# ScalarE copies for row sums, query rows and expert numbers; a search begun in the query blocks; gathers held for blocks of the down stage

## The reference, cut to what matters

```python
def peer(h, w_q, sub_keys, w_down, w_up):          # h: 256 tokens x 1024
    q = (ht @ w_q).reshape(T, 8, 2, 128)
    scores = einsum('thic,hikc->thik', q, sub_keys)   # 16 halves x 128 keys
    sv, si = lax.top_k(scores, 16)
    cand = sv[:, :, 0, :, None] + sv[:, :, 1, None, :]
    best, ci = lax.top_k(cand.reshape(T, 8, 256), 16)
    i1 = take_along_axis(si[:, :, 0], ci // 16, axis=-1)
    i2 = take_along_axis(si[:, :, 1], ci % 16, axis=-1)
    expert = (i1 * 128 + i2).reshape(T, 128)       # of 16384 experts
    gate = softmax(best, axis=-1).reshape(T, 128)
    hid = gelu(einsum('cd,ckd->ck', xb, w_down[eb]))
    return einsum('ck,ckd->cd', gb * hid, w_up[eb])
```

## Time and profile before

| what | value |
|---|---|
| median of 3 runs | 1516.04 us |
| the profiled execution | 1503.53 us |
| its span, first to last instruction | 1501.7 us |
| granted TensorE clock | 0.997 of full |
| busy: TensorE, VectorE, GpSimd, ScalarE | 1479.2, 892.0, 716.5, 473.2 us |
| moved through the DMA engines | 523.12 MB, mean 348 GB/s |

### The profile page before, as it was taken

One profiled execution on the slowest core, in us unless ns is written; L12 is line 12 of the kernel. 1 busy time (PEld: TensorE's weight loads), 2 busy tenths in 40 slices (PEclk: granted clock), 3 DMA queues, 4 the chain that ended last, 5 costly groups with the idle time before them and its releaser, 6 DMA issues.

```text
span 1501.7 us, 29008 instructions
## 1 busy us (share of the span) xinstructions
PE 1479.2 (98%) x10648; PEld 1440.7 (96%) x10648; DVE 892.0 (59%) x2921; ACT 473.2 (32%) x1184; POOL 716.5 (48%) x632
## 2 busy tenths in 40 slices
PE   8999999999999999999999999999999999999996
PEld 6889999999999999999978999999999999999996
DVE  1740999948885444444623449997588834444363
ACT  6663231248881000000055533121788500000001
POOL 6577033448994333333467831333699723332350
PEclk9999999999999999999999999999999999999998
DMA  7356999999999999999845679999999999999993
GB/s 257 133 204 235 332 339 364 409 408 342 383 389 407 416 416 417 416 417 415 360 150 200 211 244 351 349 407 408 367 375 385 383 416 415 416 417 416 417 404 141
DMA packets 126416, 523.12 MB, mean 348 GB/s; under 512 B 14816, under 2 KB 15072, under 8 KB 109536
## 3 DMA queue, kind: packets, MB, share of 16 engines
q1 hardware_dynamic: 56896, 240.27, 42.0%
q0 software_dynamic: 55296, 201.35, 34.3%
q10 hardware_dynamic: 14112, 80.04, 13.1%
HBM read 519.48 MB, written 1.05 MB: 347 GB/s over the span
## 4 chain that ended last, share of the span: by engine, by line
PE 94%; POOL 1%; DMA 1%; issue 1%; ACT 1%; DVE 1%; DVEq 0%; POOLq 0%; SPq 0%; ACTq 0%
PE ps L992 93%; POOL w_lo L605 1%; DMA spare<-in_wu 1%; PE ps L1000 1%; ACT hT_hi L707 0%; DMA raw<-in_wm 0%; DMA xs<-in_x 0%; ACT w_hi L692 0%; ACT arena L680 0%; DVE arena L1385 0%; DVE rtmp L1374 0%; DVE arena L1523 0%; POOL arena L630 0%; PE ps L1322 0%; PE ps L1120 0%
## 5 line engine op out<-in xcount | busy, mean ns | idle before, releaser
L992 PE MATMUL ps<-arena,raw 128*128 128x160 f32 (+1 forms) x2688 | 377.4, 299 | 0.2
L992 PE MATMUL ps<-arena,w_raw 128*128 128x160 f32 (+1 forms) x2688 | 377.3, 299 | 0.0
L992 PEld LDWEIGHTS ps<-arena,raw 128*128 128x128 f32 x2688 | 368.1, 190 | 0.7 <-issue 0.7
L992 PEld LDWEIGHTS ps<-arena,w_raw 128*128 128x128 f32 x2688 | 368.2, 190 | 0.0
L622 POOL DMA_INDIRECT arena<-in_up_rows,ret x192 | 188.1, 979 | 355.1 <-DVE oh_buf L1697 263.3
L622 POOL DMA_INDIRECT arena<-in_rows,ret x192 | 200.0, 1042 | 285.8 <-ACT ret L879 104.5
L1697 DVE SCALAR_TENSOR_TENSOR oh_buf<-arena,ret,oh_buf 128x1024 f32<-128x1024 f32 x126 | 161.8, 1284 | 227.9 <-DMA arena<-in_up_rows,ret 227.9
L605 POOL TENSOR_TENSOR w_lo<-raw,w_hi 128x1024 fp32r<-128x1024 f32 x80 | 194.0, 2436 | 90.8 <-PE ps L992 66.1
L992 PE MATMUL ps<-arena 128*128 128x160 f32 (+5 forms) x1336 | 184.5, 302 | 0.4 <-DMA spare<-in_wu 0.3
L992 PEld LDWEIGHTS ps<-arena 128*128 128x128 f32 (+2 forms) x1336 | 177.9, 189 | 4.0 <-issue 2.6
L1580 DVE SCALAR_TENSOR_TENSOR arena<-arena,ps 128x1024 f32<-128x1024 f32 x128 | 153.6, 1213 | 0.0
(11 more groups left out here) (149 smaller groups left out, 1780.6 us busy)
## 6 DMA issues: line engine op xcount, KB each, us to landing
raw<-in_wd SPq DMA_DIRECT2D x92, 512.0 KB, 6.8
w_raw<-in_wd SPq DMA_DIRECT2D x92, 512.0 KB, 7.6
raw<-in_wm SPq DMA_DIRECT2D x80, 512.0 KB, 3.4
low_rows<-in_wu SPq DMA_DIRECT2D x18, 1024.0 KB, 7.9
arena<-in_wu SPq DMA_DIRECT2D x18, 1024.0 KB, 7.9
arena<-in_wd SPq DMA_DIRECT2D x32, 512.0 KB, 4.9
raw<-in_wu SPq DMA_DIRECT2D x14, 1024.0 KB, 8.0
raw<-in_wu ACTq DMA_DIRECT2D x14, 1024.0 KB, 8.0
```

The source lines that it names most:

```text
L992: return nc.tensor.matmul(out, lhsT, rhs, start=start, stop=stop, skip_group_check=shared)
```

## The change

- The table `sel` and all products with it are gone. ScalarE's `take_rows` copies `gff` to both halves of banks 2 and 3 at block 8 of its loop; `take_more_picks` copies the numbers of the 32 tokens in four parts; VectorE's `find_more_rows` is gone.
- The sums of the sparse tokens are added to `xs` by VectorE. Partitions must match, so ScalarE first moves parts to the right partitions (`move_part`, and `sums_moved` for the 64 tokens) into two unused tiles `moved`. The up rows of the 32 tokens now come first (0 to 31); their moves stand in ScalarE's program between the loads of pairs 39 and 40 and between 47 and 48, the adds on VectorE behind row products 66 and 80. The adds of the 64 tokens stand at the layer's end. Tile 0 is turned back with transposes.
- The scores of the first 4 heads of tile 0 are computed ahead of query block 10 and taken by ScalarE behind its block 12; VectorE searches them at once. The search of tile 0 is split in two halves of 4 heads; dots are now spread over 20 places from the second half on, 44 of them (`EARLY`).
- Each of the first 53 gathers waits until TensorE has used a given number of down blocks (`pace`): gather q for q * 71 // 53. The pieces of numbers are handed over at blocks 4, 7, 20 and 25. The ring starts at slot 2, since slots 0 and 1 lie on tile 0's scores; gather 9 waits for these (`first_searched`).
- The gates are transposed at block 73 instead of 77, gate blocks begin at 76 instead of 80, and the dots left (52) spread over 48 blocks instead of 56 over 44.

```diff
-RING, IN_FLIGHT = 10, 5
+RING, IN_FLIGHT, RING_FIRST = 10, 5, 2
-IDS_AT = 77
-TAKE_AT = 26
-PIECES, PIECE_AT = 4, (18, 21, 24, 26)
-MORE_AT, MORE_TAKE_AT, MORE_GATES_AT = 28, 33, 40
+IDS_AT = 73
+TAKE_AT = 28
+PIECES, PIECE_AT = 4, (4, 7, 20, 25)
+EARLY_SCORES_BEFORE, EARLY_HEADS = 10, RH // 2
+SCORE_BANKS = (0, 1, 0, 1, 4, 5, 6, 7)
+MORE_AT, MORE_TAKE_AT, MORE_GATES_AT = 26, 34, 40
-G_FROM = 80
+G_FROM = 76
-SPARSE_FIRST, MORE_LAST = 18, 10
-EARLY, EARLY_PLACES = SPARSE_FIRST + MORE - MORE_LAST, 14
+SPARSE_FIRST, MORE_LAST = 26, 14
+EARLY, EARLY_PLACES = SPARSE_FIRST + MORE - MORE_LAST, 20
+def pace(q):
+
+    return q * (IDS_AT - 2) // (EARLY + RING - 1)
-    return (True, n - PICKS) if n >= PICKS else (False, n)
+    return (True, n) if n < MORE else (False, n - MORE)
+PARTS_AT, LAST_PART_AT = 5, 6
+PARTS_ADDED, LAST_PART_ADDED = 66, 80
+        moved = [at(HT_AT + i * DM, DM) for i in range(2)]
...
+                    if q < EARLY + RING - 1:
+                        pool.wait_ge(w_used, l * LAYER + MIX_BLOCKS + pace(q))
...
+                    if q == RING - 1:
+                        pool.wait_ge(first_searched, l + 1)
                     if q < ROWS and more and j == 0:
-                        pool.wait_ge(more_taken, l + 1)
+                        pool.wait_ge(more_taken, PARTS * (l + 1))
...
+                act.wait_ge(rinv_done, query_norm)
+                for b in range(Q_FROM + 12, MIX_BLOCKS):
+                    high(b)
+                    if b == Q_FROM + EARLY_SCORES_BEFORE + 2:
+                        take_scores(0)
+                        take_scores(1)
...
+                def take_rows():
+                    act.wait_ge(hng_done, l + 1)
+                    act.wait_ge(pair_found, PIECES * l + PIECES // 2)
+                    for half in range(2):
+                        nc.scalar.activation(h_rows[half * SPARSE:(half + 1) * SPARSE], gff[0:SPARSE],
+                                             ACT.Copy).then_inc(h_rows_done, 1)
...
-                blocks(act, load_up_between, UP_PAIRS, UP_PAIRS * UP_CYCLES, UP_PAIRS)
+                def move_part(i, to):
+                    nc.scalar.activation(to[SPARSE:DENSE_FROM], more_sums[i * MORE:(i + 1) * MORE],
+                                         ACT.Copy).then_inc(parts_moved, 1)
+
+                blocks(act, load_up_between, UP_PAIRS, UP_PAIRS * PARTS_AT, UP_PAIRS)
+                act.wait_ge(row_used, l * GATHERS + ROWS + MORE)
+                move_part(0, moved[0])
+                move_part(1, moved[1])
+                blocks(act, load_up_between, UP_PAIRS * PARTS_AT, UP_PAIRS * LAST_PART_AT, UP_PAIRS)
+                act.wait_ge(parts_added, 2 * (l + 1))
+                move_part(3, moved[0])
+                blocks(act, load_up_between, UP_PAIRS * LAST_PART_AT, UP_PAIRS * UP_CYCLES, UP_PAIRS)
...
                 for g, chunks in enumerate(UP_BANKS):
+                    if g == 2:
+                        act.wait_ge(row_used, (l + 1) * GATHERS)
+                        for k in range(2):
+                            ks = slice(k * HALF, (k + 1) * HALF)
+                            nc.scalar.activation(moved[0][0:SPARSE, ks], sums[SPARSE:P, ks],
+                                                 ACT.Copy).then_inc(sums_moved, 1)
...
+                    if b == EARLY_SCORES_BEFORE:
+                        pe.wait_ge(subk_loaded, 16 * (l + 1))
+                        pe.wait_ge(qT_sb, 8 * l + 4)
+                        score(0, range(2 * EARLY_HEADS))
...
-                pe.wait_ge(hng_done, l + 1)
-                pe.wait_ge(sc_sb, 8 * l + 4)
-                for k in range(2):
-                    last = mm(ps[:, 2 + k, :], sparse_of, gff[:, k * HALF:(k + 1) * HALF])
-                last.then_inc(h_rows_psum, 1)
...
-                mm(ps[:, 5, 0:P], more_of, idf[:, 0, :]).then_inc(more_ids_psum, 1)
...
-                        last = mm(tile_psum(0, k)[:, o:o + P], upT[:, c, 0:P], ident[:, :], o == 0, c == DC - 1,
-                                  shared=True)
+                        last = nc.tensor.transpose(tile_psum(0, k)[:, o:o + P], upT[:, c, 0:P], ident[:, :])
...
-                pe.wait_ge(row_used, (l + 1) * GATHERS)
-                for k in range(2):
-                    for of, part in ((sparse_to, sums), (more_to, more_sums)):
-                        last = mm(tile_psum(0, k), of, part[:, k * HALF:(k + 1) * HALF], False,
-                                  of is more_to and k == 0, shared=True)
-                    if k == 0:
-                        last.then_inc(tiles_psum, 1)
...
+                search(0, 0, EARLY_HEADS, 2, 2, 3)
+                search(0, EARLY_HEADS, RH, 4, 5, 1)
+                gates_of(0)
+                search(1, 0, RH, 8, 5, 0)
+                gates_of(1)
...
                 for n in range(ROWS):
                     axpy(n)
+                    if n == PARTS_ADDED:
+                        dve.wait_ge(row_used, l * GATHERS + ROWS + MORE)
+                        dve.wait_ge(parts_moved, 3 * l + 2)
+                        for k in range(2):
+                            step(add_to(more_tokens, more_sums, k))
+                        for k in range(2):
+                            step(add_to(more_tokens, moved[0], k))
+                        for k in range(2):
+                            add_to(more_tokens, moved[1], k).then_inc(parts_added, 1)
+                    if n == LAST_PART_ADDED:
+                        dve.wait_ge(parts_moved, 3 * (l + 1))
+                        dve.wait_ge(parts_added, 2 * (l + 1))
+                        for k in range(2):
+                            step(add_to(more_tokens, moved[0], k))
+
+                def add_sparse(k):
+                    step(add_to(sparse_tokens, sums, k))
+                    dve.wait_ge(sums_moved, 2 * l + k + 1)
+                    step(add_to(sparse_tokens, moved[0], k))
+
+                dve.wait_ge(row_used, (l + 1) * GATHERS)
+                add_sparse(0)
+                if l + 1 == LAYERS:
+                    add_sparse(1)
+                settle()
                 for i, (t, k) in enumerate(((1, 0), (0, 0), (1, 1), (0, 1))):
-                    dve.wait_ge(tiles_psum, 3 * l + min(i + 1, 3))
+                    if i == 2 and l + 1 < LAYERS:
+                        add_sparse(1)
+                        settle()
+                    dve.wait_ge(tiles_psum, 2 * l + i // 2 + 1)
```

More of the change, by code:

```diff
@@ L276, in build_trunk @@
         tab = at(BS_AT, 2, TILES, ROT)
-        more_to, sparse_to, sparse_of, more_of = (sel[:, i * P:(i + 1) * P] for i in range(4))
-        part_of = sel[:, 4 * P:]
         hn = at(HN_AT, TILES, DM)
@@ L877, in take_picks @@
                         here, size = slice(half * SPARSE, (half + 1) * SPARSE), PICKS // PIECES
-                        first = half * PICKS + i * size
+                        first = (2 * i + half) * size
                         nc.scalar.activation(row_index[here, i * size:(i + 1) * size],
@@ L1171, in _, with score @@
                     transpose_half(xs, 4, hT_psum, k, HALF_BANKS)
+                def score(t, halves):
+                    for n in halves:
+                        o = n % 4 * P
+                        last = mm(ps[:, SCORE_BANKS[4 * t + n // 4], o:o + P], qT[:, n, t * P:(t + 1) * P],
+                                  subk[:, n, :])
+                        if n % 4 == 3:
+                            last.then_inc(sc_psum, 1)
                 for b in range(Q_BLOCKS):
@@ L1222, in _ @@
                     last.then_inc(w_used, 1)
-                pe.wait_ge(subk_loaded, 16 * (l + 1))
-                for t in range(TILES):
-                    for n in range(HALVES):
-                        if n % 4 == 0:
-                            pe.wait_ge(qT_sb, 8 * l + (8 if t else max(4, n // 2 + 2)))
-                        o = n % 4 * P
-                        last = mm(ps[:, 4 * t + n // 4, o:o + P], qT[:, n, t * P:(t + 1) * P], subk[:, n, :])
-                        if n % 4 == 3:
-                            last.then_inc(sc_psum, 1)
+                for n in range(2 * EARLY_HEADS, HALVES, 4):
+                    pe.wait_ge(qT_sb, 8 * l + n // 2 + 2)
+                    pe.wait_ge(sc_sb, 8 * l + n // 4 - 1)
+                    score(0, range(n, n + 4))
+                pe.wait_ge(qT_sb, 8 * (l + 1))
+                score(1, range(HALVES))
                 def down(b):
@@ L1584, in _, with early_dot, search @@
                 early = [0]
[L1586 to L1595 removed]
+                def early_dot():
+                    if not early[0]:
+                        dve.wait_ge(h_rows_done, 2 * (l + 1))
+                        dve.wait_ge(more_rows_sb, 16 * PARTS * (l + 1))
+                    dots(early_after(early[0] - 1), early_after(early[0]))
+                    early[0] += 1
+                def search(t, h0, h1, ready, bank, dots_from):
+                    heads, halves = slice(h0, h1), range(2 * h0, 2 * h1)
```

(18 more changed lines are left out.)

149 lines of the change are left out of this document (68 added, 81 removed).

## The result

The changed kernel takes 1500.03 us (median of 10 runs, 1495.44 to 1509.02), the kernel before 1514.09 in the runs beside it (10, 1510.36 to 1518.74): ratio 0.9906, 95% interval 0.9887 to 0.9926. The profiled execution took 1499.63 us, span 1497.8: only 3.9 less than the span before.

The account below looks back on a forecast made before the run. TensorE, busy 98% of the span, was taken to bound the kernel. Savings of 2 x 1.94 us in the down stages and 4.0 and 3.9 at the layer ends, about 12, gave a median of 1504.0 us, range 1500.5 to 1511.

Parts of the forecast that it names:

- The products that leave TensorE: TensorE, down stages and layer ends: products removed or made transposes save 6.0 us a layer, 12.0 in all.
- The two ends: Ends of layers 0 and 1: without TensorE's row sums they come 4.0 and 3.9 us earlier.
- ScalarE's wait: Up stage: ScalarE's loads wait for VectorE's adds behind row product 66; pair 49 still in time, 0 us, bound 0 to 12.
- rivals B and C: ScalarE's wait: B (0.10), rows stay slow, 11.6 us lost, 1515.6; C (0.07), overdue loads land together, 26 lost, 1530.
- The search: Query blocks: VectorE's search begins near 132.5, 19.4 us earlier, not held by GpSimd under the skill's rule; nothing gained.
- I take differences from the trace and set them against the median: Method: savings read from the profiled execution, 1503.53 us, are taken off the median, 1516.04, which is 12.5 more.
- I take 0, with 0 to 3 us of loss in the range: Down stage, held gathers: 422 GB/s wanted against 409 seen; no cost counted, 0 to 3 us of loss allowed.
- Weight loads run 8 blocks ahead: Down stage, not a run: a statement about weight loads beside the held gathers, whose cost is taken as 0.
- Rival D: Change does something else or gives more, by overlap with ScalarE or layer 0's start without the table: 1499 to 1501, chance 0.04.

Follow-up runs that it names:

- `up_later`: The changed kernel with its first two `w_up` loads (1 MB each) issued behind the load of block 103 instead of in block 8: 1491.71 us, ratio 0.9868.
- `sums_only`: The kernel before with only the row sums by ScalarE's moves and VectorE's adds, tile 0 turned by transposes, the more tokens' up rows first: 1509.41 us, ratio 0.9949.
- `late_parts`: The changed kernel with VectorE's adds of the moved sums behind row product 78 instead of 66: 1538.10 us, ratio 1.0168.
- `spread_first`: The kernel before with its first 49 gathers held for TensorE's blocks, one per 0.94 blocks from block 18 on: 1505.18 us, ratio 0.9957.
- `spread_twelve`: The kernel before with only its first 12 gathers held, one per 0.94 blocks from block 18 on: 1505.01 us, ratio 0.9941.
- `up_later_beside`: The changed kernel with its first two `w_up` loads behind the load of block 103, run beside the changed kernel on one chip: 1492.52 us, ratio 0.9840.
- `b_again`: The kernel before, unchanged, run once more with a second profile: 1516.95 us, ratio 0.9996.
- `no_hold`: The changed kernel without holding its first 53 gathers for TensorE's blocks; early search and five gathers in flight stay: 1497.44 us, ratio 0.9914.

## Why the prediction was wrong, point by point

**The products that leave TensorE: right.** The earlier trace rows gave 6.0 a layer, 12 in all. Without the waits at block 40 the profile shows it: the span of `up_later` is 1488.7, 13.0 less than 1501.7. The last output goes at 1482.29 instead of 1495.44. By my words the profiled execution would be 1491.5; that of `up_later` took 1490.54. `sums_only` shows 7.7 of the 12 by itself.

**The two ends: right.** I said 4.0 and 3.9. In layer 0, from the start of the third bank's matmuls to the next layer's transposes, it was 748.21 to 756.57, 8.36 us; after:

```profile
749.47 1.25 PE L1042 MATMUL ps<-arena 128*128 128x160 f32 x8
...
754.00 1.04 PE L1050 MATMUL ps<-consts,xs 128*128 128x128 f32 x8
```

4.53, so 3.83 gained. In layer 1, from the third bank to the output's issue, 1481.81 to 1495.44 is 13.63, after 1481.58 to 1491.38 is 9.80: 3.83. VectorE's adds took 0.68 us each; the 0.69 that I took as their bound stands in the trace of before (1484.52), but not in the earlier trace rows. The transposes that I put at 750.4 come at 750.07 in `up_later`; in the changed kernel they are 3.6 late, by waits in its down stage and query blocks that run 1.1 us later.

**ScalarE's wait: right, with its margin.** I put product 66 at 667 and pair 49 at 673.5.

```profile
668.80 1.28 DVE L1745 SCALAR_TENSOR_TENSOR oh_buf<-arena,ret,oh_buf 128x1024 f32<-128x1024 f32 x1 [1.56 <-issue]
...
674.38 0.34 ACTq L995 DMA_DIRECT2D operand_rows<-in_wu  x1
```

In layer 1 it is 1407.81, against 675.5 + 733.6 = 1409.1. No stall. `late_parts` shows that the mechanism of rivals B and C is real, 40 us for twelve rows, and that C's way to it, loads landing together, didn't come about.

**The search: right.** The first MAX8 stands at 134.02, in an execution that is 1.3 late; I said 132.5. It isn't held beside GpSimd:

```profile
139.17 2.40 POOL L614 TENSOR_TENSOR w_lo<-raw,w_hi 128x1024 fp32r<-128x1024 f32 x1 [0.47 <-PE ps L1042]
```

```profile
140.14 1.65 DVE L1584 MAX8 oh_buf<-arena 128x8 f32<-128x128 f32 x8
```

Eight take 1.65 us, as in the earlier trace rows, though all but the last 0.22 us lies inside GpSimd's instruction. The rule that the forecast cites from the Trainium skill (SBUF — State Buffer, Who interferes with whom) agrees.

**"I take differences from the trace and set them against the median": the first step that failed.** I had noted 12.5 us between the profiled execution and the median and asked nothing of it. The profile was an execution without the gaps; common ones have them in one or both layers, up to 6.7 us each, and the change removes them. `spread_first` gives 6.5 us for them alone by its ratio; there `up_later` is 20.0 less than before by its ratio, 12 + 6.5 and 1.5 more. `spread_twelve` gives 8.9 on another chip. On the last chip, where the kernel before took 1516.65, `up_later_beside` is 24.3 less; 12 for the products leaves 12 for the gaps, by subtraction, since no run there shows them alone.

**"I take 0, with 0 to 3 us of loss in the range", of the held gathers: the second.** The sum had 241 + 181 GB/s against 409 and "Weight loads run 8 blocks ahead". It left out the 2 MB of `w_up` in SyncE's queue at the place where the gathers now start, and took the total for the share: beside a full queue of gathers SyncE's gets half, 204 GB/s, where its loads want 241. Its lag reaches TensorE at block 40, the first with only eight blocks of lead. With the lower clock that comes behind it in some executions, and smaller waits, that costs 10 to 11 us on the last chip and 5.5 to 7.3 on the one before, not 0 to 3. `up_later` shows that the 2 MB are what makes TensorE wait: with them moved and nothing else, block 40 begins without a wait.

The two errors have nearly the same size and opposite sign: on the last chip, by the ratios, 12 for the products, 12 for the gaps and 10 lost again make the 14 of the changed kernel there. As the 12 of the gaps is itself a difference, this is the account and no check of it. So the total came close by luck, though the sum of the products was right. Rival D had the time (1499 to 1501) for other reasons.

**Open:** why TensorE and VectorE step by 0.72 or 1.44 us in the burst, and why SyncE and ScalarE go on up to 3.6 us late before it. TensorE and VectorE wait for no semaphore that the profile shows there. Instructions that come late beside the gathers' transfers would fit engines pausing together, but the rows speak against it: the trace has two queues of instruction packets, and in `b_again` neither is served between 196 and 214 us, while TensorE is back at full pace at 210.31. Late signals between engines would fit SyncE and ScalarE; no run tried it. Also open is why the burst does it in nearly every execution and didn't in my first profile.

## What to carry to other kernels

When the profiled execution is far from the median, the difference is a finding: profile the kernel before once more and look for its place before any sum is made. Read the clock's column beside the idle time: a pause of 3 us in `b_again` was followed by as much again at half speed, yet a wait of 3.78 us in `no_hold` was not, so no fixed price can be put on a pause. And count traffic for each queue, not in total: beside a full second queue the first had half here, so what isn't urgent (here 2 MB, needed 120 blocks later) goes where it delays nothing; that alone was worth another 5 to 11 us.

## What the runs showed that I had not expected

A burst of five gathers behind a pause of the gather queue goes with two compute engines pausing that wait for nothing, 3.0 us of gaps and 3.4 us by the clock, and with SyncE and ScalarE going on 2.9 us late before them, in nearly every execution. Holding twelve gathers back, one per block, removed the gaps. A full queue of gathers and a full queue of block loads shared the transfer time 52.7% to 50.3%, and this sharing, not the total of 409 GB/s, set when a load landed (15.3 us after issue).
